# Query, key and value slabs of a fused transformer block in a new order, with five accumulator banks and doubled norm scratch

## What is computed

```
h  = rms_norm(x, g_mix)
proj = h @ w_in                   # q_a,k_a,v_a | q_b,k_b,v_b | gate_a,gate_b
qa, ka, qb, kb = per-head rms_norm of each (64 wide), times q_norm/k_norm
ya = block-sparse causal attention (8 heads), yb = window-128 GQA (8 q heads, 2 kv heads, sinks)
x  = x + (sigmoid(ga+b) * (ya @ w_branch_a) + sigmoid(gb+b) * (yb @ w_branch_b)) @ w_out
x  = x + relu(rms_norm(x, g_ffn) @ w_ff1)**2 @ w_ff2
```

## Time and profile before

| | us |
|---|---|
| median of 3 runs | 724.69 |
| the profiled execution, whole | 726.15 |
| its span in the profile | 724.4 |
| PE matmul busy | 709.8 (98%) |
| DVE, ACT, POOL busy | 382.3, 312.3, 331.8 |
| first stage, from the first weight product to the first score product | 6.05 to 125.80 |

### The profile page before, as it was taken

The page is one execution under the profiler, slowest core; times in us unless marked ns, Lnnn a source line. Parts: engine busy times, 40 slices in busy tenths (PEclk is TensorE's granted clock), DMA queues, the critical chain, the costliest instruction groups (busy, mean ns, idle before and its releaser), DMA issues.

```text
span 724.4 us, 9461 instructions
## 1 busy us (share of the span) xinstructions
PE 709.8 (98%) x3434; PEld 580.1 (80%) x3434; DVE 382.3 (53%) x551; ACT 312.3 (43%) x572; POOL 331.8 (46%) x207
## 2 busy tenths in 40 slices
PE   8898999999999999899999999999999999999998
PEld 6686888888888888787888888888888888888887
DVE  5786653455445453886875521255113551166787
ACT  7575773566656554553443411333212431233220
POOL 4464664455554444343344454344444344344442
PEclk9999999999999999999999999999999999999999
DMA  8221333222221211442322322322322322322231
GB/s 272 85 88 59 111 102 111 75 73 75 86 80 54 88 58 59 138 142 99 108 96 90 114 87 93 111 87 87 116 87 87 110 93 87 115 88 88 89 115 58
DMA packets 22910, 69.89 MB, mean 96 GB/s; under 512 B 2731, under 2 KB 4267, under 8 KB 22876
## 3 DMA queue, kind: packets, MB, share of 16 engines
q1 hardware_dynamic: 22876, 69.44, 29.1%
HBM read 67.27 MB, written 2.16 MB: 96 GB/s over the span
## 4 chain that ended last, share of the span: by engine, by line
PE 88%; DVE 7%; ACT 1%; DMA 1%; issue 1%; SPq 1%; DVEq 0%; ACTq 0%
PE bank L882 27%; PE bank L883 26%; PE bank L884 26%; PE bank L996 3%; PE bank L1007 2%; DVE probs L800 2%; PE bank L1024 2%; PE bank L1026 1%; DVE store L617 1%; DMA w_raw<-slabs 1%; DVE probs L790 1%; DVE x_lo L802 1%; DVE probs L788 1%; DVE store L621 1%; ACT x_hi L542 1%
## 5 line engine op out<-in xcount | busy, mean ns | idle before, releaser
L308 POOL TENSOR_TENSOR w_lo<-w_raw,w_hi 128x1024 fp32r<-128x1024 f32 x111 | 268.3, 2417 | 295.8 <-ACT w_hi L369 295.8
L882 PE MATMUL bank<-x_hi,w_hi 128*128 128x512 f32 (+1 forms) x600 | 237.5, 396 | 3.4 <-DVE x_lo L608 2.1
L883 PE MATMUL bank<-x_lo,w_hi 128*128 128x512 f32 (+1 forms) x600 | 232.6, 388 | 0.0
L884 PE MATMUL bank<-x_hi,w_lo 128*128 128x512 f32 (+1 forms) x600 | 232.5, 387 | 0.0
L369 ACT ACTIVATE w_hi<-w_raw 128x1024 fp32r<-128x1024 f32 x112 | 118.5, 1058 | 142.2 <-PE bank L884 142.2
L882 PEld LDWEIGHTS bank<-x_hi,w_hi 128*128 128x128 f32 x600 | 113.0, 188 | 34.9 <-issue 5.1
L884 PEld LDWEIGHTS bank<-x_hi,w_lo 128*128 128x128 f32 x600 | 113.0, 188 | 23.6
L883 PEld LDWEIGHTS bank<-x_lo,w_hi 128*128 128x128 f32 x600 | 113.1, 188 | 21.4
L882 PE MATMUL bank<-qk_hi,w_hi 128*128 128x512 f32 x320 | 125.9, 394 | 1.8 <-DVE w_lo L796 1.8
L884 PE MATMUL bank<-qk_hi,w_lo 128*128 128x512 f32 x320 | 125.3, 391 | 0.0
L883 PE MATMUL bank<-qk_lo,w_hi 128*128 128x512 f32 x320 | 125.1, 391 | 0.0
(11 more groups left out here) (103 smaller groups left out, 649.4 us busy)
## 6 DMA issues: line engine op xcount, KB each, us to landing
w_raw<-slabs SPq DMA_DIRECT2D x112, 512.0 KB, 3.3
store<-x_t SPq DMA_DIRECT2D x16, 256.0 KB, 2.8
bias_m<-tab_dram SPq DMA_DIRECT2D x8, 256.0 KB, 4.5
out<-store SPq DMA_DIRECT2D x7, 256.0 KB, 2.0
bias_m<-tab_dram SPq DMA_DIRECT2D x8, 128.0 KB, 3.8
w_raw<-slabs SPq DMA_DIRECT2D x2, 384.0 KB, 5.7
w_raw<-slabs SPq DMA_DIRECT2D x2, 128.0 KB, 4.4
out<-store SPq DMA_DIRECT2D x2, 128.0 KB, 1.7
```

The source lines that it names most:

```text
L308: pool.tensor_tensor(w_lo[:, g % WS, :], w_raw[:, g % RAW, :], w_hi[:, g % WS, :].bitcast(F32), ALU.subtract).then_inc(w_lo_ready, 1)
L882: pe.matmul(out_, wh, xh, start=first, stop=False)
L883: pe.matmul(out_, wh, xl, start=False, stop=False)
L884: last = pe.matmul(out_, wl, xh, start=False, stop=end)
```

## The change

The slabs are ordered k, q, q, v, q, v, q, v (all of branch B but two of A's values), then k, q four times, then the last two values. `acc(g)` takes banks 0, 1, 2, 6, 7 in turn. `sq_hi`, `sq_lo`, `sq`, `mean_sq`, `root` and `root_sq` have two buffers each, chosen by the slab's number modulo 2; `fix` has one. The mean square of x is a product at the end of slab 2 and goes to bank 5. `split_hi(g + 2)` stands ahead of the squares of slab g on ACT throughout. The bias products stand in slabs 10 and 11, and attention starts after only the five head pairs of branch B have their low part.

```diff
-QKV_KIND = ["k", "q", "q", "q", "q", "v"] + ["k", "q"] * 4 + ["v"] * 4
-QKV_TILE = [0, 1, 2, 3, 4, 0] + [5, 9, 6, 10, 7, 11, 8, 12] + [1, 2, 3, 4]
+QKV_KIND = ["k", "q", "q", "v", "q", "v", "q", "v"] + ["k", "q"] * 4 + ["v"] * 2
+QKV_TILE = [0, 1, 2, 0, 3, 1, 4, 2] + [5, 9, 6, 10, 7, 11, 8, 12] + [3, 4]
...
-        sq, mean_sq, root, root_sq, fix = (store[:, j, :] for j in (14, 15, 8, 7, 9))
+        sq, mean_sq = [store[:, j, :] for j in (14, 3)], [store[:, j, :] for j in (15, 0)]
+        root, root_sq = [store[:, j, :] for j in (8, 1)], [store[:, j, :] for j in (7, 2)]
+        fix = store[:, 9, :]
-        sq_hi, sq_lo = pt_hi[:, 0, :], pt_lo[:, 0, :]
+        sq_hi, sq_lo = [pt_hi[:, j, :] for j in (0, 1)], [pt_lo[:, j, :] for j in (0, 2)]
...
-            return bank[{3: 5, 4: 6, 5: 7}.get(g, g % 3)]
+            return bank[(0, 1, 2, 6, 7)[g % 5]]
...
+            split_hi(3)
+            qkv_square(0)
+            qkv_square(1)
+            for g in range(2, N_QKV):
+                split_hi(g + 2)
+                if not is_v(g):
+                    qkv_square(g)
                 if g == 2:
+                    qkv_root(0)
+                    qkv_root(1)
+                if g == 3:
+                    qkv_hi(0)
+                    qkv_hi(1)
+                if g >= 4 and not is_v(g - 2):
+                    qkv_hi(g - 2)
+                if g >= 6 and is_v(g - 1):
+                    v_hi(g - 1)
+                if g == 5:
+                    v_hi(3)
+                if g >= 3 and not is_v(g - 1):
+                    qkv_root(g - 1)
+                if g == 3:
                     act.wait_ge(ms_ready, 1)
                     power(r_root, r_root_sq, r_inv_sq, r_root_ready, 3)
...
+            for g in range(2, N_QKV):
+                if g in (10, 11):
+                    table_half(g - 10)
+                if g == 4:
                     dve.wait_ge(r_root_ready, 3)
                     refine(r_all[:, :], r_root, r_root_sq, r_inv_sq, r_ready, 2)
+                    v_scale(3)
+                if not is_v(g):
+                    qk_split_squares(g)
+                elif g > 3:
+                    v_scale(g)
...
+                if g >= 3 and not is_v(g - 1):
+                    qk_norm(g - 1)
+                if not is_v(g):
+                    qk_mean(g)
...
-            AFTER = {2: 7, 3: 6, 4: 5, 5: 6, 6: 7, 7: 7, 8: 5, 9: 4, 10: 4, 11: 4, 12: 4, 13: 4, 14: 4}
+            AFTER = {(3, 0): 0, (3, 2): 1, (3, 6): 2, (5, 4): 3, (5, 5): 4}
+            AFTER.update({(g, 5): g - 1 for g in range(6, N_QKV)})
...
-                    if g == 2 and kt == 2:
+                    if (g, kt) == (2, KT - 1):
                         pe.wait_ge(xsum_ready, KT - 1)
-                        mean_square(x_sum, bank[6]).then_inc(ms_done, 1)
-                        after(0)
+                        mean_square(x_sum, bank[5]).then_inc(ms_done, 1)
...
-            pe.wait_ge(qk_lo_ready, N_QK)
+            pe.wait_ge(qk_lo_ready, qk_count(FIRST_A))
+            pe.wait_ge(ss_read, N_QK)
```

More of the change, by code:

```diff
@@ L430, in qkv_root @@
-            def qkv_root(g):
[L431 to L445, removed]
-                if g == 2:
[L447 to L451, removed]
-                if g == 3:
[L453 to L461, removed]
+                n, t = qk_count(g), QKV_TILE[g]
@@ new lines, in qkv_hi, with v_hi @@
+                act.wait_ge(pre_ready, n + 1)
+                act.activation(qk_hi[:, t, :], pre[n % 2], ACT.Copy).then_inc(qk_hi_ready, 1)
+            def v_hi(g):
+                act.wait_ge(vt_done, v_count(g) + 1)
+                act.activation(v_parts[:, QKV_TILE[g], :, 0::2, :],
+                               bank[5][:, :].rearrange("p (t e d) -> p t e d", t=QT, e=2),
+                               ACT.Copy).then_inc(v_hi_ready, 1)
+            def qkv_root(g):
+                n = qk_count(g)
+                act.wait_ge(ss_read, n + 1)
+                if n >= 2:
+                    act.wait_ge(fix_ready, 2 * (n - 1))
+                power(root[n % 2], root_sq[n % 2], mean_sq[n % 2], root_ready, 3 * n + 3)
@@ new lines, in qk_mean @@
+            def qk_mean(g):
+                n = qk_count(g)
+                dve.wait_ge(ss_done, n + 1)
+                if n >= 2:
+                    dve.wait_ge(fix_ready, 2 * (n - 1))
+                dve.scalar_tensor_tensor(out=mean_sq[n % 2], in0=r_inv_sq, scalar=EPS, in1=bank[3 + n % 2][:, :],
+                                         op0=ALU.mult, op1=ALU.add).then_inc(ss_read, 1)
+            def qk_norm(g):
+                n = qk_count(g)
+                dve.wait_ge(root_ready, 3 * n + 3)
+                if n:
+                    dve.wait_ge(pre_ready, n)
+                refine(fix, root[n % 2], root_sq[n % 2], mean_sq[n % 2], fix_ready, 2 * n + 2)
+                dve.wait_ge(fix_ready, 2 * n + 2)
+                if n >= 2:
+                    dve.wait_ge(qk_lo_ready, n - 1)
+                dve.wait_ge(par_ready, 2)
+                c = norm_column(g)
+                to = pre[n % 2][:, ::-1] if QKV_KIND[g] == "k" else pre[n % 2]
+                dve.scalar_tensor_tensor(out=to, in0=acc(g)[:, :], scalar=par[:, c:c + 1],
+                                         in1=fix, op0=ALU.mult, op1=ALU.mult).then_inc(pre_ready, 1)
@@ L931, in qkv_read, with table_product @@
                     pe.wait_ge(pre_ready, qk_count(g) + 1)
+            def table_product(h):
+                if h:
+                    pe.wait_ge(tab_copied, 1)
+                else:
+                    pe.wait_ge(tab_arrived, 32)
+                    pe.wait_ge(const_ready, 3)
+                    pe.wait_ge(v_lo_ready, v_count(8))
+                pe.matmul(bank[5][0:NH, :], tabw, hot[:, S * h:S * h + S], start=True, stop=True).then_inc(tab_done, 1)
             def mean_square(total, out_):
```

200 lines of the change are left out of this document (76 added, 124 removed).

## The result

The changed kernel takes 728.12 us (median of 6 runs, 727.66 to 728.52), against 725.23 us for the kernel before (6 runs, 723.51 to 726.65): a ratio of 1.0038, with a 95% interval of 1.0025 to 1.0050. That is 2.9 us more, inside the range and in the direction of the forecast (726.7 us), on the slower side of the 0.3% line. The two profiled executions are nearer to the working than the medians are: the span goes from 724.4 to 726.5 us, where the sum had said 726.4. Part of the rest may be chance: of 57 runs of the kernel before that were timed beside the experiments, the 11 with a mean granted clock of 0.999 or more took 722.5 to 723.5 us, the 36 with 0.995 or less 724.1 to 727.3 us, while all six of the changed kernel had 0.995 to 0.998.

What follows compares the result with a forecast made beforehand. PE was taken to bound the kernel, with 7.45 us of first-stage losses to win. Terms -4.7 + 4.1 - 1.7 + 1.7 + 2.8 - 1.05 + 0.8 = +2.0 us gave 726.7 us; range 721.2 to 729.0.

Steps and rivals of the forecast that it cites:

- The bound, and what could be won: PE is 88% of the chain; only its first-stage losses can move, together 7.45 us, about 1% of the time.
- Mean square at the slab's end, -4.7 us: Slabs 2 and 3: waits around x's mean square and the lower clock go, 1.2 + 1.8 + 1.7 us.
- The wait in slab 5, +4.1 us: First transposes, due 42.2, wait until 46.3 for value scaling, as POOL holds DVE's refinement of x's norm.
- the clock's fall, +1.7 us: Slab 5: after 3.9 us of PE idle time the granted clock falls; bounds 0 and 1.7 us.
- Rival A: Slab 5: DVE gets the ports before POOL for x's refinement; 720.9 us, or 722.4 with one operation held; chance 0.2.
- Rival B: Slab 5: the clock stays at 2.4 GHz; 725.0 us; chance 0.1.
- Weight copy ahead of the squares, seven waits of 0.4 us, +2.8 us: Slabs 7, 9, 12 to 16: sums due 4.08 us after slab start, DVE's split done at 4.37.
- 0.08 us for the start after a drained pipeline: Part of the 0.4 us cost at each of seven sums, beside 0.32 us.
- The end of the stage, +0.8 us: Gate slab waits for its bank behind slab 15's norm, held by POOL's `qk_lo`; 0 to 1.5 us.
- Double buffers, 0: The waits that double buffers and five banks remove end no idle time of PE: counted 0.
- Rival C: Slabs 12 to 16 and tail grow 0.35 us each as the cycle passes 6.3 us: 729 us; chance 0.15.

Runs made afterwards that it cites:

- the mended kernel: Changed kernel with x's root, refinement and value scaling ahead of slab 2's norm, sums from slab 6 behind kt 6, another bank for slab 15: 718.0 us.
- the filled wait: Changed kernel with 16 more products of 128x512 on PE in slab 5's wait, into bank 5: 726.49 us.
- the late weight copy: Changed kernel with ACT copying slab 6's weights behind slab 4's squares and slab 2's high part: 725.39 us.
- x's root first: Changed kernel with x's root, refinement and value scaling ahead of slab 2's root and norm, slab 4's sums behind kt 6 of slab 5: 721.34 us.
- later sums: Changed kernel with sums of key or query slabs behind kt 6 instead of kt 5, from slab 6 on: 725.44 us.
- the run with the squares first: Changed kernel with ACT squaring key or query slabs ahead of copying the next weights again, from slab 6 on: 727.17 us.
- single buffers: Changed kernel with one buffer again for squares and norm scratch from norm number 5 (slab 8) on: 728.23 us.
- the early mean square: Changed kernel with the mean square of x back behind kt 2 of slab 2: 732.09 us.

## Why the prediction was right

- *The bound, and what could be won.* Right. The forecast counted 7.45 us of losses in the first stage; the mended kernel has no wait there and is 7.2 us faster than the one before. Of the 7.45 us, 1.7 us are the clock behind slab 2, which one execution showed.
- *Mean square at the slab's end, -4.7 us.* Right in mechanism. The last addition ends near where the walk put it (25.13 for 25.5, with a start 0.26 us earlier), held by POOL, and no wait follows. The size was not measured as a whole: putting the product back costs 4.0 us, of which 2.3 us are its wait, but leaves the sums of slab 0 where they are now.
- *The wait in slab 5, +4.1 us, and the clock's fall, +1.7 us.* Right in mechanism and size: 4.13 us, and 1.5 us by the rows of the filled wait. That the refinement held by POOL makes the wait is shown by the late weight copy, with which the two operations take 0.68 and 0.69 us; x's root first takes the wait away though they are held, by starting them 2.8 us sooner (38.28 for 41.11). Rival A (DVE first at the ports) had a margin of 0.6 us in the working and of 0.49 us in the trace, and did not come. Rival B (the clock stays high) did not either: no run of the changed kernel has a mean clock above 0.998.
- *Weight copy ahead of the squares, seven waits of 0.4 us, +2.8 us.* The mechanism and the places are right, the size was short: a period of 6.36 us is 0.46 us over, 3.2 us in all. The term that was low is "0.08 us for the start after a drained pipeline": the step behind each restart is 0.34 us, 0.11 over, and the next few are 0.23 to 0.24 us. The later sums take all seven waits away. That POOL holds the split is read from the rows: 2.03 us, ending 0.55 us after POOL (99.53 and 100.08), against 0.67 us at 90.62 in the run with the squares first, ahead of POOL's start at 91.10. Putting ACT's order back does not do it everywhere, as that run shows.
- *The end of the stage, +0.8 us.* 0.64 us of idle time, 0.7 us with the drain, behind one refinement operation held by POOL (1.78 us). Another bank for slab 15 takes it away.
- *Double buffers, 0.* Right in the steady part.
- *Rival C (the steady part falls behind).* It did not come. The cycle held with a period of 6.36 us, and even at 5.9 us with later sums. With the squares first, a pattern of every second slab came instead.

The sum on the trace was +2.0 us of span and the trace shows +2.1, in two executions that both have the lower clock once in the first stage and once in the branch stage. That so good an agreement came out is in part luck: the term of the clock could have been 0 in either. The forecast of 726.7 is 1.4 us under the measured median, 0.5 us because the median of before is 725.2 us by more runs instead of 724.7, and 0.9 us because the medians differ by 2.9 us and not by 2.0; chance in the granted clocks may be part of that, which is not shown.

## What to carry to other kernels

An operation of DVE with both inputs in SBUF must be costed with POOL's timeline beside it: where POOL began first in these traces, it lasted to POOL's end plus 0.55 us, and in a chain the two take turns, so two operations of 0.69 us became 4.1 us here. When a step is moved ahead, follow also the operation that now stands behind it: the late weight copy cut one wait from 4.0 to 1.3 us and made another of 1.1. And where a result comes 0.3 us too late in every period, asking for it one tile later cost nothing here, while speeding up its chain moved the collision to every second slab. And before a difference of 1 or 2 us is laid to a change, look whether the granted clock fell in the same places in both executions.

## What the runs showed of the hardware that I had not expected

- The clock's fall is fixed neither by the idle time nor by the kernel. The 1.83 us of idle time in the branch stage were followed by the lower level in five of the ten profiled executions (before, the change, the filled wait, x's root first, all three mended) and by none in the other five.
- Behind the same 4.0 us in slab 5 the fall came at different places: at 46.0 us, as PE resumed, in the changed kernel; at 44.7, while it was idle, with the sums later; at 47.8, 1.2 us after it had resumed, with single buffers. PE then worked for about 3.3 us at the lower level in the first and the third, and for some 5.5 us in the second and with the early mean square. The 2.2 us of idle time of that last one were followed by no fall, nor were the waits of 1.3 and 1.1 us with 2.5 us between their ends, while 1.05 and 1.62 us were in the kernel before.
- A short wait costs PE more than its row says: 0.17 us in the list of waits, 0.46 us in the period, of which 0.16 us is the end of the product before it and 0.11 us the longer step behind it.
